# Two square output projections by halves of the tokens: the weights of each fetched and split twice, and the norm of the first four token tiles placed inside the second half

## What is computed

```python
def _rms_norm(x, g):
    y = xf * lax.rsqrt(jnp.mean(xf * xf, axis=-1, keepdims=True) + EPS)
    return (y * g).astype(x.dtype)
...
    for layer in range(DEPTH):
        xn = _rms_norm(x, g[0])
        if layer < N_A:
            mix = _short_conv(xn, conv_in_w, conv_w, conv_out_w)      # ends in  (...) @ w_out
        else:
            mix = _dilated_attention(xn, q_w, o_w, shared, slopes)     # ends in  (...) @ w_o
        x = x + _rms_norm(mix, g[1])
        ff = _swiglu(_rms_norm(x, g[2]), ffn_in_w[layer], ffn_out_w[layer])
        x = x + _rms_norm(ff, g[3])
```

## Time and profile before

| | us |
|---|---|
| three executions | 2391.96, 2392.87, 2396.44 |
| median | 2392.87 |
| profiled execution, span from first to last instruction | 2391.2 |
| PE busy | 2280.6 (95%) |
| DVE busy | 1487.9 (62%) |
| ACT busy | 937.3 (39%) |
| POOL busy | 498.8 (21%) |

### The profile page before, as it was taken

One profiled execution on the slowest core, in us unless ns is written; L12 is line 12 of the kernel. 1 busy time (PEld: TensorE's weight loads), 2 busy tenths in 40 slices (PEclk: granted clock), 3 DMA queues, 4 the chain that ended last, 5 costly groups with the idle time before them and its releaser, 6 DMA issues.

```text
span 2391.2 us, 31917 instructions
## 1 busy us (share of the span) xinstructions
PE 2280.6 (95%) x10792; PEld 1897.1 (79%) x10792; DVE 1487.9 (62%) x2212; ACT 937.3 (39%) x1706; POOL 498.8 (21%) x431
## 2 busy tenths in 40 slices
PE   7999996999999999989999999989789999999998
PEld 6888784788888888877888888878578888888886
DVE  5333317766666667796655666563586667666768
ACT  4111115322322244564555555562443223323444
POOL 1000007423232101241000000000653333320103
PEclk9999997999999999999999999999889999999999
DMA  4111110333333377635332332223023333337774
GB/s 142 47 51 52 53 53 7 100 97 111 111 109 97 119 266 241 210 111 159 80 80 59 73 76 65 64 54 115 27 86 114 101 102 97 102 106 258 248 237 163
DMA packets 240243, 265.57 MB, mean 111 GB/s; under 512 B 18016, under 2 KB 157280, under 8 KB 238048
## 3 DMA queue, kind: packets, MB, share of 16 engines
q1 hardware_dynamic: 237152, 252.25, 34.9%
q10 hardware_dynamic: 2944, 11.53, 1.3%
HBM read 189.81 MB, written 48.76 MB: 100 GB/s over the span
## 4 chain that ended last, share of the span: by engine, by line
PE 85%; DVE 5%; issue 4%; ACT 2%; POOL 2%; DMA 1%; SPq 1%; DVEq 0%; ACTq 0%; POOLq 0%
PE banks L950 35%; PE banks L1001 15%; PE banks L789 11%; PE banks L1046 8%; PE banks L890 7%; PE banks L1085 2%; PE banks L1098 2%; PE banks L1112 2%; PE banks L1124 1%; PE banks L835 1%; DVE down_split L1897 1%; DVE xn L1781 1%; POOL rstd L2326 1%; DVE bias L2171 0%; ACT pt L1577 0%
## 5 line engine op out<-in xcount | busy, mean ns | idle before, releaser
L950 PE MATMUL banks<-xb,up_split 128*128 128x512 f32 x3696 | 847.2, 392 | 12.0 <-DVE xb L1739 12.0
L950 PEld LDWEIGHTS banks<-xb,up_split 128*128 128x128 f32 x3696 | 699.1, 189 | 157.9 <-issue 12.4
L1001 PE MATMUL banks<-down_split 128*128 128x512 f32 x1848 | 422.4, 390 | 3.3 <-DVE down_split L1897 2.4
L1001 PEld LDWEIGHTS banks<-down_split 128*128 128x128 f32 x1848 | 345.7, 188 | 78.1 <-DVE down_split L1897 6.7
L1897 DVE TENSOR_TENSOR down_split<-down_raw,down_split 128x1024 fp32r<-128x1024 f32 x154 | 198.0, 1285 | 102.3 <-ACT down_split L1418 102.0
L1418 ACT CAST down_split<-down_raw 128x1024 fp32r<-128x1024 f32 x154 | 162.0, 1053 | 211.4 <-PE banks L1001 174.0
L1798 DVE TENSOR_TENSOR up_split<-sums,up_split 128x512 fp32r<-128x512 f32 x176 | 154.3, 878 | 130.1 <-ACT up_split L1319 130.0
L1046 PE MATMUL banks<-x_hi,w_second 128*128 128x512 f32 x672 | 196.9, 407 | 0.0
L2442 POOL TENSOR_TENSOR sums<-raw_up 128x512 f32<-128x512 f32 x88 | 118.6, 1350 | 369.3 <-DMA raw_up<-in_ffn_in_w 165.5
L789 PE MATMUL banks<-x_hi,w_first 128*128 128x512 f32 x768 | 184.7, 392 | 1.2 <-ACT x_hi L1264 1.1
L789 PEld LDWEIGHTS banks<-x_hi,w_first 128*128 128x128 f32 x768 | 144.9, 189 | 32.0 <-issue 1.5
(11 more groups left out here) (163 smaller groups left out, 3206.2 us busy)
## 6 DMA issues: line engine op xcount, KB each, us to landing
raw_up<-in_ffn_in_w SPq DMA_DIRECT2D x88, 512.0 KB, 5.2
down_raw<-in_ffn_out_w SPq DMA_DIRECT2D x154, 256.0 KB, 3.4
down_raw<-hid_spill SPq DMA_DIRECT2D x154, 256.0 KB, 4.2
hid_spill<-hid_mix SPq DMA_DIRECT2D x110, 256.0 KB, 2.5
down_second<-in_ffn_out_w SPq DMA_DIRECT2D x66, 256.0 KB, 3.2
k_stack<-k_parts SPq DMA_DIRECT2D x32, 512.0 KB, 6.2
raw_first<-in_conv_in_w SPq DMA_DIRECT2D x24, 512.0 KB, 3.7
hid_spill<-hid SPq DMA_DIRECT2D x44, 256.0 KB, 2.4
```

The lines of the kernel that those rows point to most:

```text
L950: mm = pe.matmul(bank(b_out), up_split[:, p, a, q * P:(q + 1) * P], xb[:, RIGHT_OF[p], b, q, :], start=(i == 0), stop=(i == len(passes) - 1))
L1001: mm = pe.matmul(bank(b_out), side[:, a, 0, i * P:(i + 1) * P], side[:, b, 1, :], start=(p in (M3, M5, M1, M2) and first and j == 0), stop ...
```

## The change

`token_product` now runs over 16 chunks: chunks 0 to 7 for tiles 0 to 3 (both output halves), chunks 8 to 15, the same weights loaded and split again, for tiles 4 to 7. A chunk is now 24 matmuls and no longer 48. The norm of tiles 0 to 3 is spread over chunks 8 to 11 on ACT and DVE (`STEPS_AT`) and runs freely on POOL; PE turns these tiles at four points of chunks 9 to 11 (`NORM_TURNS`), and their normed values go to the place of `mix`. The norm of tiles 4 to 7 follows behind chunk 15, as before, tile by tile. In the second layer the attention's tiles 4 to 7 are turned inside chunks 0 and 1 (`OUTPUT_TURNS`). Banks and block buffers are laid out anew to make this possible. POOL's four weight sums of the first column tile lie now among the norm of tiles 4 to 7 and the low parts of the blocks.

```diff
-    chunks = {"conv_in": 3 * KT, "conv_out": KT, "attn": 3 * PAIRS, "oproj": KT}
+    chunks = {"conv_in": 3 * KT, "conv_out": 2 * KT, "attn": 3 * PAIRS, "oproj": 2 * KT}
...
+        OUTPUT_TURNS = {(0, 1): HT, (0, 3): HT + 1, (1, 1): HT + 2, (1, 3): HT + 3}
+        NORM_TURNS = {(KT + 1, TT - 1): 0, (KT + 2, HT + 1): 1, (KT + 2, TT - 1): 2, (KT + 3, HT + 1): 3}
+        STEPS_AT = {KT: (0, 1), KT + 1: (2, 3), KT + 2: (4, 5), KT + 3: (6, 7, 8)}
...
                 for c in range(2 * KT):
                     weights(c + 1, ph)
+                    for t in range(c // KT * HT, c // KT * HT + HT):
+                        tile_chunk(c, t)
+                        if ph == "oproj" and (c, t) in OUTPUT_TURNS:
+                            turn_output(OUTPUT_TURNS[c, t])
+                        if (c, t) in NORM_TURNS:
+                            turn(norm_ph, NORM_TURNS[c, t])
...
             def up_layer(ph, norm_ph):
-                for t in range(HT + 2):
+                for t in range(HT, HT + 2):
                     turn(norm_ph, t)
...
+            def token_product(ph, norm_ph):
+                for c in range(2 * KT - 2):
+                    if c or ph == "conv_out":
+                        prepare(chunk0[ph] + c + 2)
+                    for i in STEPS_AT.get(c, ()):
+                        norm_step(norm_ph, 0, i)
+                    if c % KT == HT - 1:
+                        if c < KT:
+                            dve.wait_ge(post_in, 16 * posts[norm_ph])
+                        for t in range(c // KT * HT, c // KT * HT + HT):
+                            take_output(ph, 0, t)
+                for i in range(HT + LAG[norm_ph][3]):
+                    norm_step(norm_ph, HT, i)
...
+            def mixer_norm(ph):
+                first_means(AFTER[ph], 0)
+                norm_steps(ph, 0, range(HT + 2))
+                first_means(AFTER[ph], HT)
+                norm_steps(ph, HT, range(HT))
+                weight_sums(UP_OF[ph], 0, (0,))
+                norm_steps(ph, HT, range(HT, HT + 2))
+                for t in range(HT, TT):
+                    if t > HT:
+                        weight_sums(UP_OF[ph], 0, (t - HT,))
+                    sums_low(ph, t)
...
-            first_means("conv_out")
-            weight_sums("up0", 0)
-            norm("norm1")
+            norm0()
+            mixer_norm("norm1")
```

More of the change, by code:

```diff
@@ L271, in xn_tile @@
         def xn_tile(ph, t):
-            return acc_tile[t][:] if ph == "norm2" else xn[:, t % 2, :]
+            if ph == "norm2":
+                return by_tile(acc_tile[t][:])
+            if ph in OF_MIXER and t < HT:
+                return mixed(ph, t)
+            return by_tile(xn[:, t % 2, :])
         def acc_half(t, j):
@@ new lines, in turn_output, with token_product, tile_chunk @@
+                elif t == HT:
+                    pe.wait_ge(*o_done.at("attn", STEPS * PAIRS))
+                turn_tile("oturn", t, by_tile(resid[:, t, :]))
+            def token_product(ph, norm_ph, a_hi, a_lo):
+                def tile_chunk(c, t):
+                    half, q = c % KT // HT, c % HT
+                    last = q == HT - 1
+                    w_of = w_split(chunk0[ph] + c)
+                    if q == 0 and t >= HT and half:
+                        pe.wait_ge(*xl_ready.at(norm_ph, HT - 1 if t < HT + 2 else HT))
+                    elif q == 0 and t >= HT:
+                        pe.wait_ge(*mix_done.at(ph, mix_count(0, t - HT)))
+                    elif q == 0 and ph == "oproj" and half:
+                        pe.wait_ge(*xl_ready.at("oturn", TT))
+                    elif q == 0 and ph == "oproj":
+                        pe.wait_ge(*pl_done.at("attn", STEPS * PAIRS))
+                        pe.wait_ge(*xl_ready.at("oturn", min(t + 2, HT)))
+                    passes = [(a, w, k) for a, w in ((a_hi, 0), (a_hi, 1), (a_lo, 0))
+                              for k in range(2)]
+                    for i, (a, w, k) in enumerate(passes):
+                        mm = pe.matmul(bank(token_bank(ph, half, t)), a(2 * q + k)[:, t * P:(t + 1) * P],
+                                       w_of[:, w, k * HALF:(k + 1) * HALF],
+                                       start=(q == 0 and i == 0),
+                                       stop=(last and i == len(passes) - 1))
+                    if t % HT == HT - 1:
+                        mm.then_inc(chunk_done.sem, 1)
+                    elif last:
+                        mm.then_inc(tok_done.sem, 1)
+                for c in range(2 * KT):
+                    weights(c + 1, ph)
+                    for t in range(c // KT * HT, c // KT * HT + HT):
[4 more added lines that the diff above has]
+                            turn(norm_ph, NORM_TURNS[c, t])
@@ new lines, in norm0, with norm_step @@
+            def norm0():
+                _, _, _, lag_split = LAG["norm0"]
+                for i in range(TT + lag_split):
+                    if i in (TT // 2, TT // 2 + 2):
+                        prepare((i - TT // 2) // 2)
+                    if i < TT:
+                        second_square("norm0", i)
+                    if i >= lag_split:
+                        high_part("norm0", i - lag_split)
+            def norm_step(ph, first, i):
+                lag1, lag2, _, lag_split = LAG[ph]
+                if first and i == HT:
+                    act.wait_ge(*chunk_done.at(AFTER[ph], 2 * KT))
+                    up_high(UP_OF[ph], 0)
+                    up_high(UP_OF[ph], 1)
+                if i < HT:
+                    t = first + i
+                    token_finished(act, AFTER[ph], 1, t)
+                    square(bank(token_bank(AFTER[ph], 1, t)), square1[:, t:t + 1], sq1_done, ph)
+                    last_square.append(sq1_done.at(ph, t + 1))
+                if 0 <= i - lag1 < HT:
+                    left_scaled(ph, first + i - lag1)
+                if 0 <= i - lag2 < HT:
+                    second_square(ph, first + i - lag2)
+                if 0 <= i - lag_split < HT:
+                    blocks_high(ph, first + i - lag_split)
@@ new lines, in norm0, with norm_step @@
+                    if 0 <= i - lag_xn < TT:
+                        normed("norm0", i - lag_xn)
+            def norm_step(ph, first, i):
+                lag1, _, lag_xn, lag_split = LAG[ph]
+                if first == 0 and i == 0:
+                    dve.wait_ge(pre_in, 16 * pres[ph])
+                    if ph == "norm3":
+                        dve.wait_ge(x_back, 16)
+                if first and i == HT:
+                    up_low(UP_OF[ph], 0)
+                    up_low(UP_OF[ph], 1)
+                if i < HT:
+                    take_output(AFTER[ph], 1, first + i)
+                if 0 <= i - lag1 < HT:
+                    right_added(ph, first + i - lag1)
+                if 0 <= i - lag_split < HT:
+                    blocks_low(ph, first + i - lag_split)
+                if 0 <= i - lag_xn < HT:
+                    normed(ph, first + i - lag_xn)
@@ L1837, in token_product @@
                             take_output(ph, 0, t)
-            norm("norm0")
+                for i in range(HT + LAG[norm_ph][3]):
+                    norm_step(norm_ph, HT, i)
+            norm0()
             dve.wait_ge(*xt_turned.at("norm0", TT))
@@ L2327, in root, with first_means @@
                     .then_inc(rstd_sig.sem, 1)
-            def first_means(ph):
-                for t in range(TT):
+            def first_means(ph, first):
+                for t in range(first, first + HT):
                     pool.wait_ge(*sq0_done.at(ph, t + 1))
@@ L2438, in weight_sums @@
                         (2, sums[:, 1, :], a11, ALU.subtract), (3, a12, sums[:, 2, :], ALU.subtract))):
+                    if i not in which:
+                        continue
                     pool.wait_ge(*up_lo.at(ph, PRODUCTS * (n - 1) + (1, 3, 4, 7)[i]))
```

302 lines of the change are left out of this document (130 added, 172 removed).

## The result

| | before | changed |
|---|---|---|
| median of 20 executions, us | 2392.72 | 2395.95 |
| lowest to highest | 2390.36 to 2396.44 | 2394.58 to 2399.02 |
| span of the profiled execution | 2391.2 | 2397.2 |

The ratio is 1.0015 (95% interval 1.0009 to 1.0021): slower by 3.2 us, with 2.2 to 5.0 inside the interval. The middle of that lies within 0.2% (4.8 us), and the forecast was 2397.6.

The account below looks back on a forecast made before the run. PE's chain of waits was taken as the bound, with POOL and DVE nearly without slack in the tail. Two layers at +1.0 and +2.7 in layer 1 give +4.7 us on 2392.9: 2397.6 us, range 2386 to 2406.

Parts of the forecast that it names:

- The sum: Whole kernel: +2.0 us for both layers and +2.7 only in layer 1, together +4.7 us.
- Both terms of a layer: Each layer: projection's second half 8.4 us longer, tail behind it 7.4 us shorter.
- The bound of the tail: Last projection matmul to second feed-forward product, both layers: POOL's queue decides; 35.4 us instead of 42.8.
- The term of the waits: POOL's waits in the tail: 2.9 us before, 3.3 with the first weight sum's detour through ACT.
- The second half of the tokens: Projection from the end of chunk 7, both layers: four turns 4.4 us plus PE's waits for `xn` 4.0, +8.4.
- One layer: Second half of the projection and tail of one layer together: +8.4 - 7.4 = +1.0 us.
- Layer 1 alone: Only layer 1: earlier product -1.6, its two turns +2.2, chunk 3 +0.4, `g_post` ahead of chunk 6 +1.7: +2.7 us.
- the one wait near 37 us: Sign in the second projection: one wait of PE for a split near 37 us.
- Rival 1: Tail: POOL not the bound, weight sums hidden, DVE ends it; tail shrinks by 13.3 us, total 2385.8; chance 0.20.
- Rival 2: Turns of tiles 0 and 3, both layers: clock drops in new waits, 1.7 us each, 2404.4 with four; chance 0.20.
- Rival 3: Second projection: residual's return makes `g_post` or chunks 5 and 6 land 4 us later, 2401.6; chance 0.10.
- Nothing for: No cost for new bank numbers, block layout, 8 MB more of weights and the fourth weight sum.

Follow-up runs that it names:

- both experiments on the weight sums: POOL's four weight sums put back ahead of the second norm in the changed kernel: 2388.48 us; moved late, as in the change, in the kernel before: 2401.59 us.
- the kernel with early sums: The changed kernel with POOL's four weight sums in one piece ahead of the norm of tiles 4 to 7, both layers: 2388.48 us, ratio to before 0.9983.
- the small ones: The changed kernel with second splits (chunks 8 to 15, both layers) treating only 128 of 1024 columns: 2390.77 us, ratio 0.9994.
- the kernel with chunk 3 early: The changed kernel with `g_post` loaded ahead of the residual's return and chunk 3 split before turned tile 6, layer 1: 2394.33 us, ratio 1.0010.
- second trace: The changed kernel, unedited, profiled a second time: span 2394.4 us, with the drop at 290 and none at the fold.
- the two edits above: In the changed kernel's layer 1, `g_post` loaded ahead of the residual's return: 2396.00 us; on top of it, chunk 3 split earlier: 2394.33 us.

## Why the prediction was right, and where it was not

**The sum.** +4.7 us was forecast and +3.2 measured by the medians, but the stages at like clock give +6.0. Both terms of a layer had the right mechanism; that the total came out so near is in part luck, since the drop at 290 that most traces of the changed kernel miss, for which the forecast had nothing, takes some 1 us from the 6.0, and the rest of the difference is open.

**The bound of the tail, right.** The changed tail is 34.4 us, forecast 35.4. POOL's queue was the right thing to count, and both experiments on the weight sums show it. The term was mis-sized by 1.0: a sum took 1.27 us and not the 1.47 chosen between bounds (three of them, -0.6), a root 1.00 and not 1.13 (eight, -1.0), an addition 1.12 and not 1.01 (four, +0.4), and POOL's waits in the groups above sum to 3.9 and not 3.3 (+0.6). That makes 0.6 of the 1.0; the rest lies in single instructions that no group separates. The term of the waits was built wrongly, too: the idle times of the earlier trace rows sum to 4.3 and not to the 2.9 that it starts from, and the detour through ACT cost 1.8 and not 0.4; the two errors nearly cancel. For the sums the 1.28 of the earlier trace rows would have been the better choice. That they and the roots are shorter because DVE is busy for less of the tail is not shown: the addition went the other way, and in the kernel with early sums, whose DVE is busy for 25.4 of 29.5 us, a root took 0.87.

**The second half of the tokens, right in kind, too small.** +8.3 was measured in layer 0 and +8.4 forecast, but the agreement is by luck. The old projection holds a clock loss of 1.7 that this execution of the new one does not; of like executions it is 98.8 - 88.9 = 9.9. The step that failed is "the second and third turn find their `xn` ready": the second waited 1.58, as its `xn` could start only 4.7 us behind the first and took 2.02 us, and the splits were part of that (0.97 with the small ones). The first and fourth waited 2.20 and 1.80, where 2.2 and 2.2 less 0.4 in sum were forecast, so the waits are 5.6 and not 4.0. The 2.2 of the first turn is itself an error of adding: 7.9 + 2 x 0.69 + 2 x 1.14 + 1.45 + 0.5 is 13.5 and not 13.1, and the wait by these terms 2.6. With it the sum would have been +0.4 a layer, +5.5 in all.

**One layer** was put at +1.0 and is +1.6 at like clock: tail 1.0 better, projection 1.6 worse.

**Layer 1 alone** was put at +2.7 and is 4.4 - 1.6 = 2.8 us more than layer 0. The early start gave 1.8 (1.6 forecast) and its two turns cost 2.1 (2.2). For splits PE waited 0.38, 1.04 and 0.26 us (chunks 3, 5, 6) in the first profiled execution, 0.36, 0.95 and 0.88 in the second and 0.35, 1.26 and 0.57 in the third, 1.7 to 2.2 in all, where 0.4 and 1.7 were forecast, 0.9 of them from chunk 5. It was not the one wait near 37 us of the forecast's signs but three, at 22, 34 and 40 us. The load of chunk 5 took 9.9 us, the 9.1 of the earlier trace rows and a little, and the gain 17.6 for the 16.9 there. So both mechanisms were there. The prediction laid the 1.7 on the gain; the runs lay most of it on the late load of chunk 5: with the gain ahead of the return PE still waits 1.25 us for that chunk, and layer 1 gets 0.6 to 1.0 shorter, and with the load asked for early as well 3.1.

**Rival 1** (POOL not the bound) is refuted for the changed tail, but its number is worth a note: 13.3 us less tail is just what the tails give once the weight sums are away.

**Rival 2** (the clock falls in the new waits) happened in both layers, and its price was wrong. The forecast had put the four waits at no cost of clock, as lying between the 2.5 and 1.6 us of the earlier trace rows. The clock fell behind turn 0 in layer 1 of all three traces and in layer 0 of the second, and 1.6 to 1.7 us were lost each time, as priced; behind the shorter waits of the second and fourth turn it never fell. But PE had 1.58 us to wait at the next turn anyway, and the slower matmuls filled them: the projection of layer 0 is 98.8 us with the drops at 290 and at turn 0 (second trace) and the same 98.8 with that at 290 alone (the kernel with chunk 3 early), so the net price is about 0.1. That it would be the whole 1.7 with no wait behind it is what the drop at 290 shows, which costs 1.6.

**Rival 3** (the return holds up the second projection more) did not come: the gain took 0.7 us longer to land than in the earlier trace rows and the load of chunk 5 0.8, not 4. The load of chunk 6 did take 12.6 us, 3.5 more than there, yet PE waited for that chunk for 0.26 to 0.88 us and not for 4: what the load took longer was mostly hidden. What the return costs is in the forecast's own term, and can be taken away by asking for the load of chunk 5 first.

**Nothing for** the bank numbers, the layout, the fourth weight sum and the 8 MB more of weights: the stages between are as long on average (1193.3 us in three traces of either kernel), and in layer 0, where no other transfer is under way, no first-half chunk was waited for. In layer 1 the traffic did have a price, the one above.

## What to carry to other kernels

When a change halves the work behind a barrier, list in order what stays in the bounding engine's queue and look for anything moved in from its idle time: here three weight sums of 1.3 us and one detour took 5 of 13 us. A turn or any other instruction placed into a dense PE stretch belongs behind the moment its input is ready, not behind the moment its input's work starts; two tiles later took away 3.9 of 5.6 us. Compare two profiled executions only stage by stage and with equal clock drops: the same kernel's span moved by 4.5 us.

## What the runs showed of the hardware

**An equal gap drops the clock in one execution and not in the next, and the loss is the same.** The 1.88 us gap at the fold dropped the clock in two of three traces of the kernel before and in two of three of the changed one; the 2.5 us gap ahead of the first projection in all three and one of three. Over the traces of all runs, the 2.5 us gap dropped it in 11 of 13 and the 1.9 us gap in 8 of 13; PE's wait of 2.2 us at turn 0, in the changed kernel and the edits that leave it so, in 8 of 12, and the sixteen waits of 1.6 to 1.8 us at the second and fourth turn in the same runs never. Each drop took 1.6 to 1.7 us of matmul time, whatever the gap's length. What was left of it at the end of the layer differed: 1.6 for that at 290, 1.1 to 1.5 for that at the fold (135.5 against 134.2, 139.7 and 140.1 against 138.6), 0.1 for that at turn 0. The Trainium skill (TensorE: Matmul & The Clock Gate, "The HAM clock gate") says that the activity window runs freely and that the moment of a clock change varies with where in it the first matmul lands. The traces agree in kind: the same gap in the same kernel came out both ways.

**POOL and DVE lengthen each other.** In the changed tail a block part took 1.27 us when it started ahead of DVE's `xn`, and 2.27 when it started while that `xn` ran, which itself took 1.96 where others took 1.27:

```profile
405.93 1.27 POOL L2463 TENSOR_TENSOR xb_low<-t,xb_low 128x512 fp32r<-128x512 f32 x1
406.32 1.96 DVE L1850 SCALAR_TENSOR_TENSOR xn<-resid,rstd,g_pre 128x1024 f32<-128x1024 f32 x1
407.15 2.27 POOL L2463 TENSOR_TENSOR xb_low<-t_tile,xb_low 128x512 fp32r<-128x512 f32 x1
```

The Trainium skill (SBUF — State Buffer, "SBUF: two separate sides") says that the port pair which the two engines share is an exclusive lock, held for a whole instruction, when a DVE instruction with two SBUF inputs meets a POOL instruction that reads SBUF, as here. By that page `xn` would start in earnest when the first block part ends, and the second block part when `xn` ends. The rows agree: from 407.20 to 408.28 and from 408.28 to 409.42 are 1.1 us each, close to either's undisturbed 1.27. A mean duration of POOL thus holds what DVE happened to run beside it: a root took 1.13 us in the old tail, 1.00 in the changed and 0.87 in that with early sums.

**A load of 512 KB beside a 4 MB return on another queue** took 9.9 to 12.6 us to land in the changed kernel, 10.1 to 13.0 in the two edits above and 9.1 at the most in the kernel before, against 3.6 to 3.8 in quiet. The small load of the gain took 17.6 us behind the return on the same queue and 4.2 ahead of it, while the return itself went from 16.5 to 18.5 us.
